# A two-block transformer on one core: stage boundaries rebuilt (row scales behind the matmuls, output units bank by bank, first units tile by tile)

## The chip, the core and the metric

The kernel runs on one core of a Trainium2 chip. TensorE multiplies matrices into PSUM, VectorE and ScalarE work elementwise on SBUF and PSUM, GpSimd does a few elementwise operations and some DMAs, and the queue of SyncE issues the weight loads. The metric is device time in microseconds; before the change it is 2071.95 us, the median of three runs (2069.97 to 2077.83). TensorE's clock has two levels, 1.2 and 2.4 GHz; the profile shows the granted clock as a share of the higher one.

## What is computed

256 tokens of 1024 features go through two layers of a first model and two layers of a second, all in fp32. Shortened:

```python
h = layer_norm(x)
for l in range(2):                       # first block
    h = layer_norm(ALPHA * h + mixer(h) @ w_out[l])        # convolution, GQA, SGU and MLA branches
    up = depthwise_conv(h @ ffn_w_up[l])                   # width 3, 5632 columns
    h = layer_norm(ALPHA * h + (silu(up[..., :2816]) * up[..., 2816:]) @ ffn_w_down[l])
x = h
for i in range(2):                       # second block; rms_norm(x) = x * rsqrt(mean(x*x) + 1e-6) * gain
    x = x + 0.5 * swiglu(rms_norm(x), ffn1_wi[i], ffn1_wo[i])
    x = x + (ssd_pool_mixer, swa_attention)[i](rms_norm(x))
    q = rms_norm_per_head(rms_norm(x) @ xattn_wq[i])       # 4 heads of 256
    x = x + softmax(q @ mem_k.T / 16) @ mem_v @ xattn_wo[i]
    x = x + 0.5 * swiglu(rms_norm(x), ffn2_wi[i], ffn2_wo[i])
```

## The kernel before

The stream `x` lies token-major in SBUF, two row tiles `tt` of 128 tokens by 1024. Each weight matrix comes in units of 1 MB through a ring of three `raw` buffers. A unit is split into two fp32r parts: ScalarE rounds it to `w_hi` (`split`, 128x2048), then VectorE subtracts it to `w_lo`. Every product is three matmul passes (hi x hi, hi x lo, lo x hi). Splits run up to two units ahead of TensorE; the split of the second unit of a stage is done on VectorE at the boundary (`split_late`).

A stage begins with its input feature-major: `xt_hi` and `xt_lo`, eight tiles `k` of 128 features by 256 tokens. `turn` transposes `z` (the normalised stream) in 16 transposes into banks 0 to 3 (bank k // 2), `take_stream` on ScalarE makes the high parts with the gain as a scale per partition, `take_stream` on VectorE the low parts. `pair_fm` or `up_pair` then multiplies one unit: first all eight `k` of the left 128 columns, then all eight of the right ones (48 matmuls of 256 columns, `feature_major`).

A stage ends with `out_rows` or `down`: each unit adds 24 matmuls of 512 columns to banks 4 to 7, one bank for each row tile `tt` and half `h`. Within a unit the order is row tile, then the unit's two 128-row parts, then half. After the last unit `residual` (VectorE) adds each bank to `x`.

Between the two lies a norm. In the first block (`norm` with tag mix or ffn) it is a LayerNorm: bn_stats, bn_aggr, square root on ScalarE, `z` = (x - mean) / deviation, and GpSimd (`apply_wide`, four operations of 128x1024) multiplies `z` by the gain and adds the bias to make the next residual `x`, as soon as `z` is there. After the last such norm VectorE does this itself, and an RMS norm follows. In the second block it is an RMS norm: ScalarE squares and sums each row tile, root, VectorE reciprocal and scaling into `z`.

In a feed-forward stage 11 chunks of 256 columns follow each other: gate unit, up unit, and the down unit of the chunk before. In the second block ScalarE takes Silu straight from the gate's bank, VectorE multiplies by the up bank and splits the product. In the first block a convolution of three taps lies in front. Cross-attention (`xattn`) projects queries (four units), normalises each head with `head_norm` (squares, mean by a matmul, root, reciprocal of 128x256 on VectorE, product), then does four heads of scores, exponentials, transposes and values.

The order on every engine is the order of the code; semaphores do the rest.

Of the kernel before, what the change touches and what calls it, by code (L numbers as in the profile page):

```python
# [22 lines left out]
ALU = mybir.AluOpType  # L23
# [221 lines left out]
def attention_heads(kind, buf, l=0):  # L245
# [22 lines left out]
    else:  # L268
        for h in range(MEM_HEADS):
# [5 lines left out]
                out=(0, 128), tile=2 * h, first=True, last=True, scale=1.0 / 16, slope=None, h=h))  # L275
# [7 lines left out]
def mixed_block_kernel(nc, inp, consts, mem_dram, out, upto=None):  # L283
# [6 lines left out]
    with ExitStack() as ctx:  # L290
# [33 lines left out]
        rsum = sb("rsum", [P, 2, TT])  # L324
        zero = sb("zero", [P, HALF], mybir.dt.bfloat16)
# [170 lines left out]
        stored = sem("stored")  # L496


        RESIDUAL = {("mix_norm_2", l): (f"ffn1.{l}", 0.5) for l in range(2)}
        RESIDUAL |= {("xattn_norm_2", 0): ("ssd.out", 1.0), ("xattn_norm_2", 1): ("swa.out", 1.0)}  # L500
        RESIDUAL |= {("ffn2_norm_2", l): (f"xo{l}", 1.0) for l in range(2)}
        RESIDUAL |= {("ffn1_norm_2", 1): ("ffn2.0", 0.5), ("store", 0): ("ffn2.1", 0.5)}
        RESIDUAL |= {("mix", l): (f"m{l}.out", None) for l in range(2)}
        RESIDUAL |= {("ffn", l): (f"conv{l}", None) for l in range(2)}


# [77 lines left out]
        def _(pe):  # L584
# [44 lines left out]
            def stream_tile(k):  # L629

                while stream_due and stream_due[0][0] <= k:
                    taken(stream_due.pop(0)[1])
# [18 lines left out]

            def pair_fm(unit, b, name):

                w = weights(unit, (KT, 256))
                dst = claim(b, name)
                first = First()
                for j in range(2):
                    ins = feature_major(dst[:, T * j:T * j + T], w, P * j, P, first)
                ins.then_inc(bank_full[b], 1)
# [10 lines left out]
            def turn(src, tag):  # L670
# [3 lines left out]
                for tt in range(TT):  # L674
                    pe.wait_ge(z_ready, seen.next(z_ready))
                    for k in range(KT):
                        ins = pe.transpose(bank[k // 2][:, T * (k % 2) + P * tt:T * (k % 2) + P * tt + P],  # L677
                                           src[:, tt, P * k:P * k + P], ident)
                        if tt == TT - 1 and k % 2:
                            ins.then_inc(bank_full[k // 2], 1)  # L680

            def turned(tag):

                assert not stream_due
                stream_due.extend((2 * b, f"{tag}.t{b}") for b in range(4))
# [3 lines left out]
            def out_rows(units, tag, bias=None):  # L689
# [9 lines left out]
                for u, unit in enumerate(units):  # L699
# [4 lines left out]
                    for tt in range(TT):  # L704
                        for r in range(2):
                            for h in range(2):
                                b = 4 + 2 * tt + h
                                for p, (s, v) in enumerate(PASSES):
                                    ins = first(mm(bank[b][:, :], act[s][:, u % 2, r, P * tt:P * tt + P],  # L709
                                                   w[v][:, r, HALF * h:HALF * h + HALF],  # L710
# [1853 lines left out]
```

## Time and profile before

| | |
|---|---|
| time, median of 3 | 2071.95 us (2069.97 to 2077.83) |
| profiled execution: span | 2080.7 us, 31025 instructions |
| TensorE busy | 1932.7 us (93%) |
| VectorE busy | 1285.5 us (62%) |
| ScalarE busy | 892.0 us (43%) |
| GpSimd busy | 101.8 us (5%) |
| chain that ended last | TensorE 84%, VectorE 10%, ScalarE 3%, GpSimd 1% |
| mean granted clock of TensorE | 0.933 |

The chain is followed back from the last instruction, at each step to what released it. A stage is long (some 190 us for a feed-forward), so the 40 slices of the page hide the boundaries; they have to be read in windows of 20 to 40 us. In the chain "PE bank L639" are projection matmuls, L799 and L709 output matmuls, and each row gives the start, the length and the work.

### The profile page before, as it was taken

To read this page: it belongs to the slowest core of one execution; us is meant where nothing else is said; L and a number is where in the kernel's file an instruction comes from. 1 tells how busy PE (TensorE), PEld (TensorE's weight loads), DVE (VectorE), ACT (ScalarE), POOL (GpSimd) and SP (SyncE) were. 2 spreads that over 40 slices of the span, in tenths; PEclk is the share of its full clock that TensorE was granted. 3 is DMA by queue.
4 is the path that set the end of the run, shared out by engine and by line. 5 is a ranking of instruction groups with operands and counts; after the bars stand their busy time and mean duration, and the time that the engine had idled before them with its cause. 6 is when DMAs were issued, how large, how long until landed. Compare 5 with 4: busy or idle time off the path is not lost.

```text
span 2080.7 us, 31025 instructions
## 1 busy us (share of the span) xinstructions
PE 1932.7 (93%) x12412; PEld 1724.3 (83%) x12412; DVE 1285.5 (62%) x1559; ACT 892.0 (43%) x1076; POOL 101.8 (5%) x79
## 2 busy tenths in 40 slices
PE   7989799978979997999988999999999988999999
PEld 7966699976679997998986788999899875688998
DVE  5786877777687776555646556555555557565555
ACT  5444444434444443334543354333433444444332
POOL 0300200020020000000041000000000000000000
PEclk9987899988889998999986999999999995899999
DMA  9531355542135554555531434555455430224553
GB/s 299 186 111 50 134 182 181 183 133 102 61 122 182 188 189 131 185 190 168 161 105 61 142 142 151 189 185 181 162 182 182 164 119 21 100 87 160 187 189 126
DMA packets 226642, 310.78 MB, mean 149 GB/s; under 512 B 6598, under 2 KB 199398, under 8 KB 225926
## 3 DMA queue, kind: packets, MB, share of 16 engines
q1 hardware_dynamic: 223750, 298.06, 42.4%
q0 software_dynamic: 2528, 10.14, 1.5%
q10 hardware_dynamic: 288, 1.52, 0.2%
q8 instruction: 53, 0.87, 0.2%
q14 instruction: 23, 0.19, 0.0%
HBM read 306.56 MB, written 3.15 MB: 149 GB/s over the span
## 4 chain that ended last, share of the span: by engine, by line
PE 84%; DVE 10%; ACT 3%; issue 1%; POOL 1%; DMA 0%; DVEq 0%; ACTq 0%
PE bank L639 47%; PE bank L799 17%; PE bank L709 7%; PE bank L648 3%; PE bank L864 2%; PE bank L836 2%; DVE w_lo L1655 2%; DVE work L1652 1%; DVE x L1652 1%; PE bank L850 1%; DVE work L1655 1%; ACT mix L1303 1%; PE bank L1108 1%; ACT w_hi L1193 1%; DVE work L2231 1%
## 5 line engine op out<-in xcount | busy, mean ns | idle before, releaser
L1655 DVE TENSOR_TENSOR w_lo<-raw,w_hi 128x2048 fp32r<-128x2048 f32 x280 | 646.3, 2312 | 513.2 <-ACT w_hi L1193 513.0
L1193 ACT ACTIVATE w_hi<-raw 128x2048 fp32r<-128x2048 f32 x280 | 533.2, 1905 | 813.0 <-PE bank L639 532.4
L639 PE MATMUL bank<-xt_hi,w_hi 128*128 128x256 f32 x2752 | 791.8, 288 | 37.0 <-DVE xt_lo L1655 24.9
L639 PE MATMUL bank<-xt_lo,w_hi 128*128 128x256 f32 x2752 | 785.8, 286 | 0.0
L639 PE MATMUL bank<-xt_hi,w_lo 128*128 128x256 f32 x2752 | 785.4, 285 | 0.0
L639 PEld LDWEIGHTS bank<-xt_hi,w_hi 128*128 128x128 f32 x2752 | 535.4, 195 | 47.0 <-DVE xt_lo L1655 17.0
L639 PEld LDWEIGHTS bank<-xt_lo,w_hi 128*128 128x128 f32 x2752 | 535.3, 195 | 3.1 <-issue 0.7
L639 PEld LDWEIGHTS bank<-xt_hi,w_lo 128*128 128x128 f32 x2752 | 534.9, 194 | 0.0
L799 PE MATMUL bank<-w_hi,act_hi 128*128 128x512 f32 x528 | 206.4, 391 | 0.0
L799 PE MATMUL bank<-w_lo,act_hi 128*128 128x512 f32 x528 | 206.2, 390 | 0.0
L799 PE MATMUL bank<-w_hi,act_lo 128*128 128x512 f32 x528 | 205.4, 389 | 0.0
L799 PEld LDWEIGHTS bank<-w_hi,act_lo 128*128 128x128 f32 x528 | 99.1, 188 | 21.1
L799 PEld LDWEIGHTS bank<-w_hi,act_hi 128*128 128x128 f32 x528 | 99.4, 188 | 19.8 <-DVE act_lo L1655 0.9
L799 PEld LDWEIGHTS bank<-w_lo,act_hi 128*128 128x128 f32 x528 | 99.4, 188 | 18.3
L1652 DVE SCALAR_TENSOR_TENSOR work<-bank,par,work 128x255 f32<-128x255 f32 (+2 forms) x212 | 92.4, 478 | 25.7 <-ACT work L1342 18.4
L1193 ACT ACTIVATE work<-bank 128x512 f32<-128x512 f32 (+6 forms) x96 | 51.5, 545 | 117.0 <-PE bank L850 56.3
L709 PE MATMUL bank<-w_hi,act_hi 128*128 128x512 f32 x224 | 89.5, 399 | 6.7 <-ACT work L1475 3.0
L709 PE MATMUL bank<-w_lo,act_hi 128*128 128x512 f32 x224 | 88.8, 397 | 0.0
L709 PE MATMUL bank<-w_hi,act_lo 128*128 128x512 f32 x224 | 88.7, 396 | 0.0
L836 PE MATMUL bank<-work 128*128 128x256 f32 (+3 forms) x192 | 64.5, 509 | 19.9 <-DVE work L1655 9.1
L1342 ACT ACTIVATE work<-bank,par 128x256 f32<-128x256 f32 x88 | 44.5, 555 | 64.6 <-PE bank L639 64.6
L677 PE MATMUL bank<-con,mix 128*128 128x128 f32 x192 | 34.2, 341 | 40.4 <-DVE mix L1824 26.0
(256 smaller groups left out, 1874.0 us busy)
## 6 DMA issues: line engine op xcount, KB each, us to landing
raw<-in_ffn_wi SPq DMA_DIRECT2D x88, 1024.0 KB, 5.0
raw<-in_ffn_w_up SPq DMA_DIRECT2D x44, 1024.0 KB, 5.1
raw<-in_ffn_wo SPq DMA_DIRECT2D x44, 1024.0 KB, 4.8
raw<-in_ffn_w_down SPq DMA_DIRECT2D x22, 1024.0 KB, 5.3
raw<-in_w_in SPq DMA_DIRECT2D x14, 1024.0 KB, 5.3
raw<-in_ssd_in_proj SPq DMA_DIRECT2D x14, 1024.0 KB, 5.1
raw<-in_mem_wkv SPq DMA_DIRECT2D x9, 1024.0 KB, 8.4
raw<-in_w_out SPq DMA_DIRECT2D x8, 1024.0 KB, 5.0
```

The costliest lines, as they stand in the source:

```text
L639: ins = first(mm(dst, w[s][:, k, c0:c0 + m], xt[v][:, k, :], start=k == 0 and p == 0, stop=k == KT - 1 and p == 2))
L648: ins = first(mm(dst, xt[s][:, k, P * tt:P * tt + P], w[v][:, k, c0:c0 + n], start=start and k == 0 and p == 0, stop=k == KT - 1 and p == 2))
L677: ins = pe.transpose(bank[k // 2][:, T * (k % 2) + P * tt:T * (k % 2) + P * tt + P], src[:, tt, P * k:P * k + P], ident)
L709: ins = first(mm(bank[b][:, :], act[s][:, u % 2, r, P * tt:P * tt + P], w[v][:, r, HALF * h:HALF * h + HALF], start=u == 0 and r == 0 and ...
L799: ins = first(mm(bank[b][:, :], act[s][:, c % 2, j, P * tt:P * tt + P], w[v][:, j, HALF * h:HALF * h + HALF], start=False, stop=True, skip ...
L836: ins = mm(bank[b][:, at:at + n], d["q"][t][c], d["k"][c][:, 0:n], start=c == 0, stop=c == len(d["k"]) - 1)
L850: ins = pe.transpose(bank[b][:, dst:dst + P], prob[:, h % prob.shape[1], d["at"][t] + P * s:d["at"][t] + P * s + P], ident)
L864: ins = mm(bank[b][r:r + m, T * c + q0:T * c + T], v[s], prob_t[:, h % 2, T * s:T * s + T - q0], start=s == 0, stop=s == TT - 1 or d["keys ...
L1193: return act.activation(dst, src, ACT.Copy)
L1342: ins = act.activation(dst[:, c % 2, j, :], bank[b][:, T * j:T * j + T], ACT.Identity, scale=par[:, cw, at], bias=par[:, cb, at])
L1652: return dve.scalar_tensor_tensor(out=out, in0=in0, scalar=scalar, in1=in1, op0=op0, op1=op1)
L1655: return dve.tensor_tensor(out=out, in0=in0, in1=in1, op=op)
```

## The change

- `turned_at`: tile k of the turned stream now lies in bank 2 (k // 4) + k % 2, so that the first four tiles need only the left half of `x`. The transposes go half a row tile at a time.
- The last output unit is done bank by bank (`rows_of` for each row tile and half; `finish_rows`), and `residual` too.
- For five norms (`DEFERRED`: before ffn2.0, ffn1.1, ffn2.1 and both cross-attentions) `x` itself is transposed, partly between the last output matmuls. The row factor is applied later: in a feed-forward it is broadcast by two matmuls (`rb`), VectorE multiplies the gate's bank by it into `f_gate` before Silu, and the residual uses half the factor (`rhalf`) in place of 0.5. In cross-attention it cancels in the head norm; the variance gets a term for it (`vcol`).
- Cross-attention has no `head_norm`: queries keep only the gain, sums of squares are matmuls of one column, and the factor per row and head (`qscale`) is the scale of the exponential.
- The first norm of the second block is merged into the LayerNorm ahead of it (`both_g`, `both_b`); VectorE makes `x` afterwards.
- `apply_wide` waits for the split of the third unit of the stage (`behind`).
- `split_late` comes after the stream's low parts (in the deferred norms between the first and second residual blocks).
- While tiles arrive, the first unit is done tile by tile for both column halves (`both_tiles`); ScalarE and VectorE take turns on the two halves of a bank.
- The last store is in four parts.

```diff
+        DEFERRED = [("ffn2_norm_2", 0), ("ffn1_norm_2", 1), ("ffn2_norm_2", 1), ("xattn_norm_2", 0), ("xattn_norm_2", 1)]
+        ORDER = [(tt, h) for tt in range(TT) for h in range(2)]
...
+            def both_tiles(dst, w, first):
...
+                for k in range(KT):
+                    stream_tile(k)
+                    for j in range(2):
+                        for p, (s, v) in enumerate(PASSES):
+                            ins = first(mm(dst[:, T * j:T * j + T], w[s][:, k, P * j:P * j + P], xt[v][:, k, :],
+                                           start=k == 0 and j == 0 and p == 0, stop=k == KT - 1 and p == 2,
+                                           skip_group_check=True))
...
+            def finish_rows(tag, bank_done):
...
+                def part(tt, h):
+                    taken(f"{tag}.{tt}{h}")
+                    turn_half(x, tt, h)
+
+                for i in range(4):
+                    bank_done(*ORDER[i])
+                    if i == 2:
+                        for b in range(4):
+                            claim(b, f"{key[0]}{key[1]}.t{b}")
+                        part(0, 0)
+                part(0, 1)
+                part(1, 0)
+                part(1, 1)
...
+                squares_of(0)
+                if (tag, l) in DEFERRED:
+                    take_stream(f"{tag}{l}", lambda k: par_col(tag, KT * l + k))
+                squares_of(1)
+                deviations(0, TT)
...
+                if (tag, l) in DEFERRED:
+                    residual(tag, l, 0, 0)
+                    late_split()
+                    residual(tag, l, 0, 1)
+                    residual(tag, l, 1, 0)
+                    residual(tag, l, 1, 1)
+                    take_stream(f"{tag}{l}", lambda k: par_col(tag, KT * l + k))
...
+                def gate(c, turn):
+
+                    b, n = names.of[f"{tag}.g{c}"]
+                    dve.wait_ge(bank_full[b], n if turn is None else turn + n)
+                    tt_(f_gate[:, c % 2, :, :], two(bank[b][:, :]), spread(rb[:, :], 2),
+                        ALU.mult).then_inc(bank_drained[b], 1)
...
                 pool.wait_ge(wide_in, seen.next(wide_in, 0))
+                pool.wait_ge(z_ready, seen.next(z_ready, z_count))
+                pool.wait_ge(unit_split, place[behind][3] + 1)
                 for tt in range(TT):
-                    pool.wait_ge(z_ready, seen.next(z_ready))
```

VectorE at the boundary from the first cross-attention layer's feed-forward (ffn2.0) to the next feed-forward (ffn1.1), before (`x` is the stream, `mix` holds `z`, `w_lo` is a weight split, `xt_lo` the low parts of the turned stream):

```order
L1652 SCALAR_TENSOR_TENSOR x<-bank,x 128x512 x4
L1823 RECIPROCAL rs<-sd 128x1
L1824 TENSOR_SCALAR mix<-x,rs 128x1024
L1823 RECIPROCAL rs<-sd 128x1
L1824 TENSOR_SCALAR mix<-x,rs 128x1024
L1655 TENSOR_TENSOR w_lo<-raw,w_hi 128x2048
L1652 SCALAR_TENSOR_TENSOR xt_lo<-bank,par,xt_hi 128x256 x8
L1655 TENSOR_TENSOR w_lo<-raw,w_hi 128x2048 x2
L1655 TENSOR_TENSOR work<-work,bank 128x512
```

and now:

```order
L1789 SCALAR_TENSOR_TENSOR x<-bank,rhalf,x 128x512
L1792 TENSOR_TENSOR w_lo<-raw,w_hi 128x2048
L1789 SCALAR_TENSOR_TENSOR x<-bank,rhalf,x 128x512 x3
L1789 SCALAR_TENSOR_TENSOR xt_lo<-bank,par,xt_hi 128x256 x8
L2033 RECIPROCAL rcol<-sd 128x2
L2035 TENSOR_SCALAR rhalf<-rcol 128x2
L1792 TENSOR_TENSOR w_lo<-raw,w_hi 128x2048 x2
L1792 TENSOR_TENSOR work<-bank,rb 128x512
L1792 TENSOR_TENSOR work<-work,bank 128x512
```

The two scalings are gone, the split has moved up among the residual blocks, the reciprocal stands behind the low parts and a product with `rb` before that with the up bank.

VectorE at the boundary from the second convolution feed-forward to the second block, from the last bn_aggr on, before:

```order
L1732 BN_AGGR mv<-bn 128x2
L1737 RECIPROCAL rs<-sd 128x1
L1738 TENSOR_SCALAR mix<-x,mv,rs 128x1024
L1655 TENSOR_TENSOR mix<-mix,wide 128x1024
L1655 TENSOR_TENSOR x<-mix,wide 128x1024
...
L1823 RECIPROCAL rs<-sd 128x1
L1824 TENSOR_SCALAR mix<-x,rs 128x1024
L1655 TENSOR_TENSOR w_lo<-raw,w_hi 128x2048
L1652 SCALAR_TENSOR_TENSOR xt_lo<-bank,par,xt_hi 128x256 x8
```

and now:

```order
L1885 BN_AGGR mv<-bn 128x2
L1979 TENSOR_SCALAR mix<-x,mv,rs 128x1024
L1889 RECIPROCAL rs<-sd 128x1
L1979 TENSOR_SCALAR mix<-x,mv,rs 128x512 x2
L1859 CAST xt_hi<-mix 128x512
L1792 TENSOR_TENSOR xt_lo<-mix,xt_hi 128x512
...
L1792 TENSOR_TENSOR w_lo<-raw,w_hi 128x2048
L1792 TENSOR_TENSOR x<-mix,wide 128x1024
L1792 TENSOR_TENSOR x<-x,wide 128x1024
...
L2033 RECIPROCAL rcol<-sd 128x2
L2035 TENSOR_SCALAR rhalf<-rcol 128x2
L1792 TENSOR_TENSOR w_lo<-raw,w_hi 128x2048 x2
```

The products with `wide` (gain and bias) have moved behind the stream and its split, but still stand ahead of the third unit's split.

TensorE from the last output unit of ffn2.0 on, now (before, 24 output matmuls were followed by 16 transposes of `mix`):

```order
L887 MATMUL bank<-w_hi,act_lo 128x512
L716 MATMUL bank<-con,x 128x128 x4
L887 MATMUL bank<-w_hi,act_hi 128x512
L887 MATMUL bank<-w_lo,act_hi 128x512
L887 MATMUL bank<-w_hi,act_lo 128x512
L887 MATMUL bank<-w_hi,act_hi 128x512
L887 MATMUL bank<-w_lo,act_hi 128x512
L887 MATMUL bank<-w_hi,act_lo 128x512
L716 MATMUL bank<-con,x 128x128 x12
L683 MATMUL bank<-xt_hi,w_hi 128x256
```

Four of the 16 transposes stand ahead of the last bank's six matmuls, and they read `x`.

## Rows read from the trace of the kernel before

**Rows 1.** Chain of the whole span; columns: start us, us, what.

```profile
1600.99 11.51 PE bank L639 x96
```

**Rows 2.** Chain around the boundary from ffn2.0 to ffn1.1.

```profile
1451.77 7.52 PE bank L799 x33
1459.32 1.38 DVE x L1652 x2
...
1461.95 1.28 ACT L1304
...
1465.96 2.20 DVE w_lo L1655
...
1469.09 11.87 PE bank L639 x96
```

**Rows 3.** Timeline there; start us, us, engine line op out<-in xcount [idle before <-releaser].

```profile
1464.67 1.06 PE L677 MATMUL bank<-con,mix 128*128 128x128 f32 x8 [1.99 <-DVE mix L1824]
...
1466.49 3.03 ACT L1221 ACTIVATE xt_hi<-bank,par 128x256 fp32r<-128x256 f32 x8 [1.52 <-PE bank L677]
1468.08 3.22 DVE L1652 SCALAR_TENSOR_TENSOR xt_lo<-bank,par,xt_hi 128x256 fp32r<-128x256 f32 x8
```

**Rows 4.** Chain around the first LayerNorm boundary (first mixer to convolution feed-forward).

```profile
208.25 1.30 DVE x L1652 x2
...
209.65 1.30 DVE bn L1730 x2
...
214.95 2.94 DVE mix L1738
...
224.75 2.72 DVE xt_lo L1655
```

**Rows 5.** Timeline at the same boundary.

```profile
214.02 0.81 DVE L1738 TENSOR_SCALAR mix<-x,mv,rs 128x1024 f32<-128x1024 f32 x1
...
214.98 2.35 POOL L2298 TENSOR_TENSOR x<-mix,wide 128x1024 f32<-128x1024 f32 x1 [67.56 <-DVE mix L1738]
...
218.66 3.76 ACT L1221 ACTIVATE mix<-bank,par 128x256 f32<-128x256 f32 x8 [4.37 <-PE bank L677]
...
227.39 0.41 DVE L1718 CAST xt_hi<-mix 128x512 fp32r<-128x512 f32 x1
...
227.84 0.69 DVE L1655 TENSOR_TENSOR xt_lo<-mix,xt_hi 128x512 fp32r<-128x512 f32 x1
```

**Rows 6.** Chain around the start of the second block.

```profile
788.15 1.24 DVE x L1655
...
795.00 13.37 PE bank L639 x96
```

**Rows 7.** Chain of the whole span: first matmuls after two LayerNorm boundaries.

```profile
227.61 13.71 PE bank L639 x96
...
434.10 23.11 PE bank L639 x168
```

**Rows 8.** Chain in the first cross-attention.

```profile
1224.31 0.60 ACT work L1193
...
1236.48 0.44 PE bank L850 x4
1236.91 1.74 PE bank L864 x8
...
1245.94 18.66 PE bank L709 x81
```

**Rows 9.** Windows at two boundaries; us, busy by engine (PE PEld DVE ACT POOL), PEclk, DMA, GB/s.

```profile
988.00:990.00 2.00, 1.09 (x8) 0.86 (x8) 2.00 (x2) 1.41 (x4) 0.00 (x0) 1.00 0.00 0
...
1196.00:1198.00 2.00, 0.80 (x4) 0.45 (x3) 2.00 (x5) 2.00 (x6) 0.00 (x0) 0.50 0.05 12
```

**Rows 10.** Timeline of VectorE in the first mixer, GpSimd working beside it.

```profile
88.33 3.98 DVE L1655 TENSOR_TENSOR w_lo<-raw,w_hi 128x2048 fp32r<-128x2048 f32 x1 [2.93 <-ACT w_hi L1193]
```

**Rows 11.** The page's costliest groups: the convolution taps and like operations.

```profile
L1652 DVE SCALAR_TENSOR_TENSOR work<-bank,par,work 128x255 f32<-128x255 f32 (+2 forms) x212 | 92.4, 478 | 25.7 <-ACT work L1342 18.4
```

More of the change, by code:

```diff
@@ L655, in pair_fm @@
                 dst = claim(b, name)
[L656 to L659, printed above, removed]
+                both_tiles(dst, w, First()).then_inc(bank_full[b], 1)
             def pair_tm(unit, b, name):
@@ L675, in turn @@
                     pe.wait_ge(z_ready, seen.next(z_ready))
[L676 to L682, printed above, removed]
-                assert not stream_due
-                stream_due.extend((2 * b, f"{tag}.t{b}") for b in range(4))
+                    for h in range(2):
+                        turn_half(src, tt, h)
@@ L687, in _, with turned @@
+            def turned(tag, biased=False):
+                assert not stream_due
+                for k in range(KT):
+                    b, half = turned_at(k)
+                    if biased and k % 2 == 0:
+                        stream_due.append((k, None))
+                    elif not biased:
+                        stream_due.append((k, f"{tag}.t{b}" if half else None))
             act = (act_hi, act_lo)
@@ L781, in ffn_any @@
                 up_pair(1, 2, None)
+                if scaled:
+                    pe.wait_ge(row_ready, seen.next(row_ready))
+                    claim(1, f"{tag}.rb")
+                    for tt in range(TT):
+                        ins = mm(bank[1][:, P * tt:P * tt + P], rcol[:, tt:tt + 1].broadcast_to([P, P]), ident,
+                                 start=True, stop=True)
+                    ins.then_inc(bank_full[1], 1)
                 for tt in range(TT):
@@ L1156, in xattn, with square_sums @@
                 turned(f"xattn_norm_2{l}")
+                def square_sums(h):
+                    pe.wait_ge(sq_ready, seen.next(sq_ready))
+                    b = 4 + h % 2
+                    claim(b, f"xn{l}.ms{h}")
+                    for tt in range(TT):
+                        for c in range(2):
+                            ins = mm(bank[b][:, tt:tt + 1], x_sq[:, 2 * h + c, P * tt:P * tt + P],
+                                     cst("mean256")[:, 0:1], start=c == 0, stop=c == 1)
+                    ins.then_inc(bank_full[b], 1)
                 for j in range(4):
@@ L1785, in residual @@
                 name, factor = RESIDUAL[tag, l]
[L1786 to L1793 removed]
+                b = full(f"{name}.{tt}{h}")
```

411 lines of the change are left out of this document (272 added, 139 removed).

## The prediction

> **What bounds the kernel now.** I read the shares of the page and its chain first: TensorE carries the chain nearly everywhere, so only places where it stands still are worth anything. In the loops of the six feed-forward stages the chain is matmuls without a gap: 96 matmuls of up-projections in 11.51 us [rows 1], then 24 of down-projection at 7.52 / 33 = 0.228 us [rows 2], 5.47 us. Nothing there can be gained. Next I read the chain across the joints. From the last output matmul (E) to the first matmul of the next stage (F) the reader should see only VectorE, ScalarE and transposes.
>
> RMS joints (seven). In the one between the two feed-forwards, [rows 2]: the last unit's first 9 matmuls end at 1459.3, when the first residual row block starts; 15 more end at E = 1459.3 + 15 x 0.228 = 1462.7. F is 1469.09, so F - E = 6.4. The other joints of this kind give the same 6.4. In it lie squares, a table load (1.28), square root, scaling, transposes, then a weight split of 2.20 that VectorE does ahead of the stream's low parts.
>
> LayerNorm joints (four; the very first stage start is covered by the memory projections). In the first [rows 4], E = 208.15 + 15 x 0.228 = 211.55, F = 227.61, so 16.1. Four VectorE instructions are stretched while GpSimd works beside them, each by 2.0 to 2.1 us; two are shown: a scaling takes 2.94 for 0.81, a subtraction 2.72 for 0.69 [rows 4, 5]; between them lie a split and a cast. Together 8.5 us. Before the second block's first norm VectorE also applies gain and bias itself (1.24 us, four times) [rows 6] and a second norm follows; F is 795.0 against E = 780.1 (the same count of matmuls after the first residual block), 14.9 us [rows 6].
>
> **The change, part by part.**
>
> A. Five RMS joints lose the norm from their path (stream turned unscaled, row factor applied behind). Work, from E of the old order: the bank-by-bank order completes the banks after 6, 12, 18, 24 matmuls in place of 9, 12, 21, 24, so the last bank is as late as before, plus the four transposes put ahead of the last group: 1.06 / 8 = 0.13 each [rows 3], 0.5 us. VectorE: block 1 at 1458.7 to 1459.4, the moved split 1459.5 to 1461.8 (its ScalarE half ends by 1459.5), blocks 2 and 3 to 1463.2, block 4 from 1463.4 (bank full) to 1464.1 (0.69 each, half of 1.38 [rows 2]). TensorE has turned tiles 0 to 3 by 1464.2. ScalarE tile 0: 3.03 / 8 = 0.38; VectorE 3.22 / 8 = 0.40 [rows 3]; two handoffs and the matmul's own: F = 1465.15 against 1469.09. Gain 3.95. Tiles then come every 0.43 (the two engines alternate over two banks) while TensorE, now taking both column halves at each tile, uses 6 x 0.12 = 0.72: no stall, where the first two units took 11.87 for 11.51, gain 0.35. Five times 4.3 = 21.5.
>
> What is late next: on ScalarE the second squares, table load and root, under 3 us, now stand between the stream and the third unit's split. They end near F + 5.5, the split's two halves by F + 9.7; TensorE wants that unit at F + 11.5 plus the zeroing matmuls. Hidden, with 3 us to spare. The row factors are then broadcast by two matmuls of 128 columns in each RMS feed-forward: nearest rows, transposes of that shape at 0.13 each and the 256-column pair of fp32 matmuls below at 0.43; I take 0.45 with the wait, bounds 0.2 to 1.0. Three joints here: -1.35. A = 20.1.
>
> B. The two RMS joints that keep their norm (before the mixers): the split leaves the path (2.20) and tiles 0 to 3 are handed over half a row block earlier, but block order costs a little: F = E + 4.35. The split then ends 0.5 us before it is wanted. Gain 2.05, twice 4.1.
>
> C. Three LayerNorm joints. VectorE in the new order, from E = 211.55: last block 212.55 to 213.2, statistics to 213.9, aggregate 214.15 (1.30 for two halves [rows 4]), first scaling 0.81 to 214.95, two half scalings to 216.0. Transposes for tiles 0 to 3 at 216.1 to 216.7, ScalarE 2 x 0.47 [rows 5], VectorE cast and subtraction 0.42 + 0.69, F = 219.0 = E + 7.45. Gain 8.6 each, 25.8. The moved split ends at F + 5.5 and is wanted at F + 5.76: just in time, bound 0 to 1 us late.
> The four GpSimd instructions are not gone but wait for the split of the third unit. In the first mixer the trace already shows them at F + 7: a split of 3.98 us for 2.29 [rows 10], and TensorE there keeps its pace, so for the second mixer I take 0. For the two convolution feed-forwards nothing shows it. From F + 7.8 VectorE has one split, 8 taps (0.48 each [rows 11]), products and operand parts (0.69 + 0.42 + 0.69) and another split before TensorE wants the first down-projection at F + 24: 10.4 of work and 8.5 of blocking in 16.2 us if everything is serial, 2.7 us too late; if the taps, which read PSUM, are not blocked, nothing. I take 0, bounds 0 to 8.5 a joint.
> The Trainium skill (SBUF — State Buffer, "SBUF: two separate sides") says that GpSimd and those VectorE operations that run in a two-port mode or read two SBUF inputs share one port pair, "an exclusive lock, not a bandwidth split". The 2.94 beside GpSimd's 2.35 agrees. The rule speaks against this part: what is moved blocks again where it lands. By it the PSUM-fed taps go free, which gives the 0; without that the sum would lose 2.7 twice.
>
> D. Before the second block: F = E + 7.45 here too, 787.55, gain 7.45. But VectorE still owes the four products (5.0 us), and ScalarE squares them before it splits the third unit: products end F + 10.5, root F + 12.1, split F + 16.3, wanted F + 13.9. So 2.1 to 2.5 us come back as a stall, and TensorE starts the third unit at F + 16.4 = 803.95 against 809.3. D = 5.4.
>
> E. Cross-attention, two. Before: from the end of the last query projection (1224.3) to the output projection (1245.94) 21.65 us [rows 8]: copy, square, mean, root, reciprocals on VectorE, products, then scores. Without head norms: square and four one-column matmuls, scores from +1.2. TensorE's own work is 4 heads x (1.74 values, as much for the scores, 0.44 transposes) = 15.7 [rows 8]; followed hand (exponential from +4.25 because the table load waits for the scores) values end at +17.7, output at +18.4. Gain 3.25. One-column matmuls are not in the trace: between 4 x 0.13 and the 0.86 of the pairs they replace (two of 256 columns, 0.43 each); I take 0.53, three more per stage, gain 1.0. E = 2 x 4.3 = 8.6.
>
> F. Clock. After long gaps the granted clock falls to half (1.2 for 2.4 GHz), seen at 1196 but not at 988 after gaps of equal length [rows 9]. First units then take 13.71 or 13.37 for 11.5, and the first 168 matmuls of the second mixer 23.11 for 20.2 us [rows 6, 7]. Outside D that is 10 us of this trace. Gaps of 2.5 us should not drop it, those of 7.5 may, as the 6.4 ones did in two of seven. I expect 3 to stay: 7.
> The Trainium skill (TensorE: Matmul & The Clock Gate, "HAM oscillation") says an idle gap re-throttles and sustained work releases. The row at 988 says a gap with transposes in it need not. By the rule each of the three remaining gaps of C costs its 2 us, 6 for my 3.
>
> Left at nothing: the gate product that replaces a read in each RMS chunk (0.69 on VectorE, which waits several us in each 16.98 us chunk; the chunk's operand is due a whole chunk later); other exponential scales; the start (second unit's split about 1 late, both halves together about 1 earlier); the smaller last transfers.
>
> Sum on the profiled execution: 20.1 + 4.1 + 25.8 + 5.4 + 8.6 + 7 = 71 off 2080.7. This execution, 2080.7 us by its span, is 8.8 longer than the median of the timed ones, though its span excludes what lies around it; that is about what the clock drops come to, so I credit the timed runs with 3 for F: 67 off 2071.95 = 2005.
>
> **Rivals.**
> 1. GpSimd's work blocks again in the open. For: the stretched rows [rows 4, 10] show blocking wherever the two meet, and VectorE is the source of each unit. Against: the first mixer. If all 8.5 us show in three joints: 2005 + 25 = 2030; if 2.7 in two, 2010.
> 2. What the joint gives is taken back by the third unit everywhere, as in D: its split stands behind second squares and root in five joints. For: D's arithmetic. Against: 3 us of slack. If ScalarE's stream is slow (each tile waiting for VectorE's, 0.8 rather than 0.43) the slack goes and each joint loses 3 to 4: 2005 + 5 x 4 + 15 for late second splits in B and C = 2040.
> 3. Slower. In the four RMS feed-forwards gate product, Silu, product, cast and subtraction become one serial chain in a loop that had no gap: 0.69 + 0.6 + 0.69 + 0.42 + 0.69 plus handoffs = 3.2 us per chunk, 44 chunks. If it lay open wholly: 141 more, 2146. It decides from 67 / 44 = 1.5 us per chunk. Against: TensorE's 16.98 us per chunk, and the operand is due more than 10 us after it is made.
> 4. It doesn't shorten: the joints' F stays because the last bank, not the norm, was late. The order above excludes it for C (8.5 us of blocking are plain).
>
> **How the numbers follow.** Forecast as worked out, with its own range 1994 to 2017: 0.74. Rival 1 0.10, rival 2 0.09, rival 3 0.04, rival 4 and other 0.03. The range goes from all terms at their good ends (square sums free, no clock drop, timed runs gain all of F: 1992) to rival 1 at full price, 2030. About 10 us is what measurement can tell from no change (0.5%). Faster holds the forecast, rivals 1 and 2: 0.94; same, a partial rival 3 or 4: 0.02; slower 0.04.
>
> **What would show it.** Between last output and first projection matmul 2.5 us in five joints, 4.4 in two, 7.5 in four; VectorE's scaling 0.81 again there; GpSimd stretching splits inside the next stage, with TensorE not waiting at the first down-projection; one wait of 2 to 3 us at the third unit of the second block's first feed-forward; 18 us from last query projection to output; loops still at 16.98. Wrong if the loops lengthen, if TensorE waits for the third unit in the five joints, or if the gaps of C exceed 9.

## The result, and the profile after

The changed kernel takes 2020.21 us (median of 4 runs, 2019.93 to 2022.33) against 2071.98 (4 runs, 2069.97 to 2077.83): 0.9749 of the time, 95% interval 0.9732 to 0.9767, so 51.8 us less, give or take 3.7. The forecast was 2005, the range 1992 to 2030. All medians here leave out one execution, of the kernel of experiment 3, that took 3779.65 us at a mean granted clock of 0.496. The profiled execution has a span of 2017.5 us, 63.2 less than that of the kernel before. The loops are what they were: in the chain of the changed kernel (start us, us, what)

```profile
1969.38 5.47 PE bank L887 x24
1974.85 11.51 PE bank L660 x96
```

11.51 us of up-projections and 5.47 of down-projection, as in [rows 1, 2]. The gate product inside the loop costs nothing.

**RMS joint without a norm in its path.** The chain of the joint between the two feed-forwards, which answers to [rows 2]:

```profile
1410.74 0.78 PE bank L716 x7
...
1411.60 0.48 ACT xt_hi L1335
...
1412.11 0.49 DVE xt_lo L1789
...
1412.63 0.48 ACT xt_hi L1335
...
1413.13 0.49 DVE xt_lo L1789
...
1413.67 6.01 PE bank L683 x48
...
1425.44 0.44 PE bank L867 x4
...
1426.85 1.15 PE bank L660 x8
```

Table load, squares, root, scaling and split are gone from it. TensorE's last transposes begin at 1410.58 in the timeline, 0.23 behind the last output matmul (the chain gives them from its end), and the next projection at 1413.67: 3.09 us, where the prediction's working gives 1.95. Before, the same distance was 6.6 (the prediction had estimated 6.4). The chain passes through two of ScalarE's tiles and two of VectorE's before TensorE moves, though its first matmul reads the first tile alone. The timeline of the same place (the bracket is the idle time before, and what ended it):

```profile
1412.11 2.68 DVE L1789 SCALAR_TENSOR_TENSOR xt_lo<-bank,par,xt_hi 128x256 fp32r<-128x256 f32 x6 [0.58 <-ACT xt_hi L1335]
...
1413.67 0.39 PE L683 MATMUL bank<-xt_hi,w_hi 128*128 128x256 f32 x1 [1.43 <-DVE xt_lo L1789]
```

VectorE makes a low tile every 0.45 us (2.68 / 6), the first by 1412.6. TensorE starts with the end of the third. The row factors' four records take 0.44 (0.45 in the prediction).

**RMS joint that keeps its norm**, before ssd, in the chain:

```profile
942.02 1.28 ACT L1424
...
943.84 0.76 DVE mix L2013
...
945.81 0.56 PE bank L716 x3
...
946.40 0.48 ACT xt_hi L1335
...
947.93 0.50 DVE xt_lo L1789
...
948.52 3.59 PE bank L669 x28
```

The last output matmul begins at 942.29 and the next instruction could follow 0.23 later, so this is 6.0 us, against 6.6 before by the same count and 4.35 in the prediction. The table load of 1.28 is still there, and where the split of 2.20 stood, transposes and tiles stand now.

**LayerNorm joint**, before the first convolution feed-forward, which answers to [rows 4, 5]:

```profile
209.48 0.69 DVE mix L1979
...
210.31 2.60 PE bank L716 x11
...
214.44 0.70 DVE xt_lo L1792
...
215.28 6.72 PE bank L683 x39
```

The subtraction of 2.72 is 0.70 again. From last output matmul (206.84) to first projection it is 8.4 us here, 7.25 and 8.0 at the next two, against 16.2 before; predicted 7.45. The transposes of this joint ran at the low clock, those of the second (7.25) at the full one. GpSimd now begins at 222.90, where it began at 214.98; the timeline there:

```profile
222.90 2.41 POOL L2523 TENSOR_TENSOR x<-mix,wide 128x1024 f32<-128x1024 f32 x1 [74.94 <-DVE w_lo L1792]
...
225.25 2.29 DVE L1792 TENSOR_TENSOR w_lo<-raw,w_hi 128x2048 fp32r<-128x2048 f32 x1 [2.52 <-ACT w_hi L1302]
...
225.39 4.40 POOL L2524 TENSOR_TENSOR x<-x,wide 128x1024 f32<-128x1024 f32 x1
...
227.46 1.78 DVE L1789 SCALAR_TENSOR_TENSOR work<-bank,par,work 128x255 f32<-128x255 f32 x4
...
232.86 2.53 DVE L1827 CAST act_hi<-work 128x512 fp32r<-128x512 f32 x1
```

Of the four only one meets VectorE at VectorE's cost here (a cast, 2.53 for 0.43). One is itself stretched, 4.40 for 2.4, by a split that began first, and the taps keep their 0.45 beside GpSimd. In the third joint a split (4.03 for 2.29) and the cast (2.52) pay. TensorE waits for none of it: from third unit to last output matmul both convolution feed-forwards take 175.43 us, before and now.

**Before the second block** the third unit is late, as forecast. In the chain:

```profile
757.73 2.37 DVE x L1792 x2
...
762.83 1.91 ACT w_hi L1302
...
764.83 2.30 DVE w_lo L1792
...
767.18 2.89 PE bank L660 x22
```

Products, squares, ScalarE's half of the split, VectorE's half, then TensorE, 15.9 us after its first projection matmul (751.31); forecast 16.4.

**Cross-attention**, in the timeline, against [rows 8]:

```profile
1176.00 1.90 PE L1262 MATMUL bank<-con,work 128*128 128x1 f32 x16
...
1188.79 0.60 ACT L1302 ACTIVATE mix<-bank 128x512 f32<-128x512 f32 x1 [1.13 <-PE bank L960]
1189.28 0.56 ACT L1520 ACTIVATE work<-bank,nmax,qscale 128x256 f32<-128x256 f32 x1
...
1191.39 0.66 PE L946 MATMUL bank<-con,work 128*128 128x128 f32 x4 [0.47 <-DVE work L2163]
...
1196.23 0.47 PE L787 MATMUL bank<-w_hi,act_hi 128*128 128x512 f32 x1 [0.73 <-issue]
```

From the last query projection (1176.00) to the output projection it is 20.2 us, against 21.65 before and 18.4 forecast. The square sums show as 16 records for two heads, 0.86 us a head, where I had put 0.53. The last head's exponential stands behind a result copy, and the output projection waits for a bank.

**Clock and the mixers.** Both mixers ended 4.4 us sooner though nothing in them was changed. In the windows of the kernel before (us, PE and PEld busy, DVE, ACT, POOL, then the granted clock) the first mixer's attention reads

```profile
160.00:170.00 10.00, 10.00 (x34) 4.49 (x32) 7.45 (x20) 2.00 (x6) 0.00 (x0) 0.50 0.01 2
```

and in those of the changed kernel

```profile
160.00:170.00 10.00, 10.00 (x45) 5.39 (x44) 7.74 (x21) 2.04 (x7) 0.00 (x0) 0.74 0.01 2
```

Half clock (1.2 GHz) through the whole window in one; in the other TensorE is back at full clock (2.4 GHz) half-way through.

### The profile page after: what moved, and what is told of

It is laid out like the page before. It is cut to its first block, busy times and chain, and to the rows that moved or that the text cites. A ratio compares the mean times of both kernels' runs of the same rounds, so it can differ in the third digit from the quotient of the medians.

```text
span 2017.5 us, 31210 instructions
## 1 busy us (share of the span) xinstructions
PE 1909.7 (95%) x12460; PEld 1712.2 (85%) x12460; DVE 1277.4 (63%) x1585; ACT 893.4 (44%) x1076; POOL 103.2 (5%) x79
## 3 DMA queue, kind: packets, MB, share of 16 engines
q10 hardware_dynamic: 288, 1.52, 0.2%
## 4 chain that ended last, share of the span: by engine, by line
PE 85%; DVE 8%; ACT 3%; issue 2%; POOL 1%; DMA 1%; DVEq 0%; ACTq 0%
PE bank L660 43%; PE bank L887 17%; PE bank L787 8%; PE bank L683 4%; PE bank L669 3%; PE bank L960 2%; PE bank L932 2%; DVE work L1789 2%; PE bank L716 1%; ACT w_hi L1302 1%; DVE w_lo L1792 1%; PE bank L946 1%; DVE work L1792 1%; PE bank L1204 1%; DVE work L2451 1%
## 5 line engine op out<-in xcount | busy, mean ns | idle before, releaser
L660 PE MATMUL bank<-xt_lo,w_hi 128*128 128x256 f32 x2560 | 725.5, 283 | 0.0
L660 PE MATMUL bank<-xt_hi,w_lo 128*128 128x256 f32 x2560 | 725.3, 283 | 0.0
L660 PEld LDWEIGHTS bank<-xt_hi,w_hi 128*128 128x128 f32 x2560 | 492.0, 192 | 6.5 <-issue 2.4
L660 PEld LDWEIGHTS bank<-xt_lo,w_hi 128*128 128x128 f32 x2560 | 491.9, 192 | 3.0 <-issue 0.7
L660 PEld LDWEIGHTS bank<-xt_hi,w_lo 128*128 128x128 f32 x2560 | 491.8, 192 | 0.0
L1789 DVE SCALAR_TENSOR_TENSOR work<-bank,par,work 128x255 f32<-128x255 f32 (+2 forms) x212 | 92.3, 478 | 23.7 <-ACT work L1477 17.3
L1302 ACT ACTIVATE work<-bank 128x512 f32<-128x512 f32 (+6 forms) x88 | 46.8, 541 | 102.9 <-PE bank L946 46.5
L683 PE MATMUL bank<-xt_hi,w_hi 128*128 128x256 f32 x192 | 59.3, 309 | 18.4 <-DVE xt_lo L1789 10.7
```

Source lines behind the costliest of these rows:

```text
L660: ins = first(mm(dst, w[s][:, k, c0:c0 + m], xt[v][:, k, :], start=k == 0 and p == 0, stop=k == KT - 1 and p == 2))
L683: ins = first(mm(dst[:, T * j:T * j + T], w[s][:, k, P * j:P * j + P], xt[v][:, k, :], start=k == 0 and j == 0 and p == 0, stop=k == KT - ...
L1302: return act.activation(dst, src, ACT.Copy)
L1789: return dve.scalar_tensor_tensor(out=out, in0=in0, scalar=scalar, in1=in1, op0=op0, op1=op1)
```

## The experiments

Times are medians; ratios are to the kernel before, with 95% intervals.

**1. The kernel before once more** (no edit): how much of the 63.2 us is one execution's clock?

> The kernel before, unchanged, profiled a second time. The two profiles differ by 63.2 us of span, the timed runs by 51.8. Theory A (the clock): about 11 us of the profiled difference is that the first profile of the kernel before held more time at the low clock level (mean 0.933), above all in the attention of the two mixers, where 32 small matmuls took 0.61 us a pair for 0.36 in the changed kernel; the timed runs hold less of it. Then this second profile has a span of about 2069 to 2072 and a mean clock of 0.937 to 0.94, and the joints' own lengths (6.4 and 16.1 us from last output matmul to first projection) are unchanged. Theory B (the changed kernel's mixers are really shorter by 4.4 us each): span again near 2080, mixers as in the first profile.

Measured: 2072.94 us, span 2070.2, clock 0.940. The window of its first mixer from 160 to 170 us:

```profile
160.00:170.00 10.00, 10.00 (x45) 5.39 (x44) 7.95 (x21) 2.01 (x6) 0.00 (x0) 0.74 0.01 2
```

It is that of the changed kernel. Theory A holds: the mixers didn't change, the first profile of the kernel before was one of its long executions. The joints have the lengths of the first profile. Its timed ones go from 2070 at a mean clock of 0.940 to 2083 at 0.934.

**2. Another bank for the first unit** behind RMS joints.

```
-claim(0, f"{tag}.g0"); up_pair(0, 0, None)
+claim(4, f"{tag}.g0"); up_pair(0, 4, None); row_factors()   # not in ffn1.0
-pair_fm(f"xq{l}.{j}", j % 2, ...)
+pair_fm(f"xq{l}.{j}", j % 2 if j else 6, ...)               # likewise ssd, swa: bank 7
```

> The changed kernel with another destination for the first unit behind an RMS joint: bank 4, 6 or 7, which the last residual has emptied, in place of bank 0, which holds the turned tiles 0 and 2 (and the two row factor matmuls between first and second unit). Theory A (destination): in the trace the first matmul starts 1.08 us after the first low tile, with the third low tile's end, because its own bank is the one those tiles are read from. Then first matmul minus last output matmul falls from 3.4 to about 2.4 us before ffn2.0, ffn1.1, ffn2.1 and both cross-attentions, the loops' third unit moves with it, 0.3 to 0.9 before ssd and swa: in all 5 to 6 us, 2020.2 to 2014.5. Theory B (the first matmul needs the tiles themselves at that pace): no change, 2020; the start moves but the first unit stretches by as much.

Measured: 2014.59 us (0.9709, 0.9683 to 0.9734), 5.6 less. In its timeline of the joint between the feed-forwards:

```profile
1414.81 0.35 PE L683 MATMUL bank<-xt_hi,w_hi 128*128 128x256 f32 x1 [0.50 <-DVE xt_lo L1796]
```

The last transposes begin at 1412.65, so 2.16 us for 3.09, and TensorE idles 0.50 for 1.43. Theory A holds. A little comes back in the first unit: at the third unit the gain is 0.99 us in cross-attention, 0.82 in the feed-forwards and 0.33 before ssd.

**3. GpSimd early again** in the changed kernel.

```
-pool.wait_ge(unit_split, place[behind][3] + 1)      # the three joints
```

> The changed kernel with one part undone: GpSimd's four gain and bias instructions start at once behind the scalings again, not behind the third unit's split. Theory A (two engines shut each other out wherever they meet): GpSimd starts near 211.4 in the first such joint; its second instruction meets VectorE's first cast (0.43 becomes 2.5), third and fourth meet a subtraction and a split. First matmul of the next stage 2.1 us later in three joints, third unit 2 to 6 later each: 2020 plus 6 to 18, so 2026 to 2038. Theory B (the new order of VectorE's own work gave the gain, the blocking is cheap): within 3 us of 2020.

Measured: 2040.76 us (four executions; 0.9848, 0.9817 to 0.9879), 20.6 more, above the range I gave. VectorE's stream in the first joint:

```profile
215.52 2.58 DVE L1859 CAST xt_hi<-mix 128x512 fp32r<-128x512 f32 x1 [2.63 <-ACT mix L1338]
218.14 2.71 DVE L1792 TENSOR_TENSOR xt_lo<-mix,xt_hi 128x512 fp32r<-128x512 f32 x1
220.78 2.60 DVE L1859 CAST xt_hi<-mix 128x512 fp32r<-128x512 f32 x1
```

Three instructions in a row pay 2.15, 2.02 and 2.18 us, together 6.35. Here two stand ahead of the first projection and the third holds up the first unit; counted at the third units, the three joints take 4.7, 6.7 and 6.5 us more, 17.8 in all. Only the first GpSimd instruction runs beside nothing. Theory A, and dearer than I had it.

**4. GpSimd late in the kernel before**, nothing else.

```
+if behind is not None: pool.wait_ge(unit_split, place[behind][3] + 1)
```

> The kernel before with that one part alone: GpSimd waits for the split of the next stage's third unit in the three LayerNorm joints. Theory A: the four stretched VectorE instructions (2.0 to 2.1 us each) were the 8.5 us; all come back at each joint and none is paid later: 2072 less 25, 2047 (from 2045 to 2051). Theory B (most of the 8 us per joint of the changed kernel came from overlapping residual, statistics and scaling): 2060 or more.

Measured: 2046.66 us (0.9874, 0.9844 to 0.9904), 26.1 less. Its chain in the first joint, with the old order of residuals, statistics and split:

```profile
209.78 0.83 DVE mix L1738
...
210.74 2.38 PE bank L677 x10
...
215.50 6.56 PE bank L639 x37
```

From the first transposes to the first projection it is 4.76 us, 4.97 in the changed kernel, both with transposes at the low clock; from the first pair of residuals (204.01) 11.5. This one wait is most of term C, and half of the whole change. In the second joint, where both kernels ran their transposes at the full clock, last output matmul to first projection is 7.8 us here and 7.25 in the changed kernel, so the finer order of VectorE's work adds 0.5. Theory A holds.

**5. The split back in the path** of the six joints that keep a norm.

```
-take_stream(...); late_split()
+late_split(); take_stream(...)
```

> The changed kernel with one part undone in the six joints that keep their norm: VectorE splits the second unit ahead of the stream's parts again, not behind them (2.2 us). Theory A (from the trace: VectorE idles 2.7 us there in the LayerNorm joints and 0.75 in the two RMS joints, waiting for transposes and ScalarE's first tile): nothing in four joints, 1.45 in two, 2020 plus 3. Theory B (the prediction's own step, 2.2 us off the path wherever the split is moved): 2.2 in six joints, 2020 plus 11 to 13.

Measured: 2023.61 us (0.9754, 0.973 to 0.9778), 3.4 more than the changed kernel. The interval doesn't tell that from nothing; the trace does. The chain before ssd:

```profile
946.23 2.20 DVE w_lo L1792
948.43 0.41 DVE xt_lo L1789
...
949.96 0.36 PE bank L669
```

From the first transposes (944.82) to the first projection it is 5.14 us for 3.78, 1.36 more; in the first LayerNorm joint 4.97 for 4.97. Theory A holds: a split of 2.2 us fills time in which VectorE would wait anyway. How much of it depends on the clock: VectorE idles 2.71 us in the first LayerNorm joint of the changed kernel, with slow transposes, but 1.52 in the second, with fast ones, and there the split costs 0.6 (4.38 for 3.78), where theory A had nothing.

**6. First units by column half again**, not tile by tile.

```
-if not stream_due:
+if True:
     for j in range(2): ins = feature_major(...)
```

> The changed kernel with the first units taken column half by column half again, not tile by tile: TensorE then uses 0.36 us per tile in the first half, under the 0.43 to 0.54 at which the tiles come. By that its first half ends with the eighth tile in place of running behind it: first unit some 0.5 to 1.0 us longer at eleven stages, 2020 plus 5 to 10 (the span of 2017.5 likewise). Rival: the first unit's start waits for a bank that is emptied with the third tile, so the stream is already ahead: under 2 us.

Measured: 2024.80 us (2 runs; 0.9761, 0.9725 to 0.9797), span 2024.5. The span's 7.0 more are mostly not this edit's: 5.7 of them are there before the first joint, where its windows show the first mixer at 0.50 and 0.57 for 0.74 and 0.92. In the joint between the feed-forwards first and second unit take 11.78 us together for 6.01 + 5.76. The rival holds there: no gain of 0.35. It does not hold where tiles come in pairs, by a cast and a subtraction of 128x512 each. The chain in the first LayerNorm joint, its first unit at full clock:

```profile
223.16 0.70 DVE xt_lo L1792
...
223.91 9.62 PE bank L660 x78
```

The first unit, begun at 220.81, is still waiting for the fourth pair of tiles; it takes 6.80 us, where the changed kernel's, at full clock in the third LayerNorm joint, takes 5.83. The first mixer's has 6.79 for 5.83 likewise. Four LayerNorm joints and the first stage are of this kind, some 1 us each, though the one before the second block waits for its third unit either way. So the median's 4.6 us, from two executions, agrees with theory A in these stages and with the rival in the rest.

**7. Square sums twice.**

```
-for tt in range(TT):
+for tt in (0, 1, 0, 1):
```

> The changed kernel with the one-column square sums of cross-attention issued twice (8 matmuls for 4 per head, same result). I had put four at 0.53 us; the trace shows 0.86 for four. Theory A (each costs 0.21 us of TensorE, set by its 128-row weight load of 0.19 and not by its one column): between the query projections 1.74 us stand in place of 0.86, so 8 x 0.87 = 7 us more in the span. Theory B (the 0.86 is mostly the switch between projections and sums, paid once): under 2 us more.

Measured: 2026.06 us (2 runs; 0.9775, 0.9753 to 0.9798), span 2023.6: 6.1 more. The span mixes in the clock (the joint before swa ran at full clock in this execution and gave 1.9 back, the first cross-attention lost some). The second cross-attention, at full clock in both, is the clean place: 3.5 us more for four heads, 0.88 for each one's four matmuls. Theory A holds; a matmul of one column costs about 0.2 us here. That its weight load sets this was not tested.

**8. All that the traces pointed to** (2, and four more edits).

```
 split(); +gate(0, None) ahead of the second split()      # ScalarE's copy of the row factors likewise
+act.activation(unused, eps[:, 0:1], ACT.Sqrt)            # at the start of each RMS joint; Exp before cross-attention
-if h >= 2: result(h - 2)
+if h >= lag: result(h - lag)                             # lag 3 in cross-attention, otherwise 2
-claim(4 + 2 * tt + h, ...) for all four, then the units
+if u == 0: claim(b, ...)                                 # each where it is first written
```

> The changed kernel with five more edits. (1) The other destination bank for the first unit behind RMS joints, measured alone at 5.6 us. (2) In those three feed-forwards the first gate product and the row factor's copy stand ahead of the second of the two splits: the third unit, which waited in the trace of the kernel with edit 1 alone for splits and gate product, starts about 0.7 us sooner. (3) The square root's table (1.28 us) is loaded by a throwaway square root at the start of each RMS joint, in ScalarE's idle time: both joints that keep their norm lose 1.28 us of path, 2.5 in all; the exponential's likewise before each cross-attention, 0.3 each. (4) In cross-attention the fourth head's exponential stands ahead of the first head's result copy: 0.5 each. (5) The output rows' accumulators are claimed when each is first written, so that the first matmul doesn't wait for the last value head's copy: 0.6 at six stages, 3.6. Sum with 5.6: 2020.2 less 15, 2005 (2001 to 2009). Rival: what edits 3 to 5 free is taken by the next wait of the same place (split of the third unit, last head's operand): 2011 or more.

Measured: 2002.49 us (0.9662, 0.9645 to 0.968), 17.7 less than the changed kernel, inside what was expected. The chain before ssd is without its table load:

```profile
942.39 0.76 DVE x L1804
...
943.23 1.16 ACT mix L1426 x2
...
944.41 0.30 ACT sd L1429
...
947.20 2.73 PE bank L670 x18
```

From the last residual (942.39) to the first projection it is 4.81 us, where the changed kernel has 5.80 (942.72 to 948.52). But the kernel of experiment 2, which still has the table load in its chain, has 4.82 (948.70 to 953.52):

```profile
953.52 0.36 PE L669 MATMUL bank<-w_hi,xt_hi 128*128 128x256 f32 x1 [0.63 <-DVE xt_lo L1796]
```

So the whole 1.0 is the other bank's, and hiding 1.28 us of table load brought nothing here: the second row tile's squares, root and scaling, which wait for the last residual, had run beside it and now are the path. The 17.7 us come from five edits at once; only the first was measured alone.

**9. Matmuls on zeros in TensorE's gaps**, in the changed kernel.

```
+busy(3, 13)      # before each LayerNorm joint's transposes
+busy(7, 9)       # behind them
+busy(0, 18)      # before each mixer's attention
```

> The changed kernel with matmuls on a tile of zeros put where TensorE waits, into banks that are empty then: 13 before the transposes and 9 behind them in each of the four LayerNorm joints, 18 before the attention of each mixer (0.21 us each at full clock). They change no result and delay nothing while they fit the gaps (3.3, 2.3 and 4.5 us). Theory A (the gaps let the granted clock fall): in the trace the granted clock stays at 1.00 at 210 to 220 and 482 to 498 us (0.53 and 0.5 to 0.57 in the changed kernel), the first unit of the first joint takes 6.0 us for 7.8, its transposes 1.3 for 2.6, and each mixer's attention is 3 to 6 us shorter: 2020.2 less 9 to 15, so 2005 to 2011. Theory B (the clock falls for another reason, or matmuls on zeros don't count): 2020 to 2023.

Measured: 2018.39 us (0.9736, 0.9721 to 0.9752), 1.8 less, where I expected 9 to 15. The joints did as theory A said (the first: transposes and first unit 1.97 and 5.89 us). The first mixer did not:

```profile
150.00:160.00 10.00, 7.97 (x23) 4.33 (x22) 9.79 (x28) 3.16 (x12) 0.00 (x0) 0.55 0.00 1
160.00:170.00 10.00, 10.00 (x35) 4.81 (x34) 7.88 (x21) 2.18 (x8) 0.00 (x0) 0.50 0.01 2
```

The clock is still up at first (0.83 from 140 to 150 us, for 0.55), falls at the attention's next wait, and stays down longer than in the changed kernel's trace (0.50 from 160 to 170 for 0.74): the output projection begins at 190.26 us for 185.0. One trace doesn't show that the zeros did the second part. From third unit to last output matmul the first mixer takes 126.5 us here, and in the twelve traces without zeros there anything from 119.4 to 125.5, three of them with 0.50 from 160 to 170 too.

**10. The edits of 8 and 9 together.**

> Both kernels' edits together. If they touch different time, the gains add: 2005 less what the filling matmuls give alone (9 to 15 by their theory A), 1990 to 1996. If they give nothing alone, 2005 to 2008.

Measured: 2001.62 us (0.9656, 0.964 to 0.9671), where 1990 to 1996 was expected. In its trace the first mixer takes 124.7 us and the second 117.7, the shortest of all.

**11 and 12. The edits of 8, and zeros in the joints alone**, twice.

> The combined kernel with the filling matmuls in the four LayerNorm joints alone, none before the mixers' attention. In the trace of the kernel with all of them the joints gained 2.8, 1.6, 1.5 and 1.2 us and both mixers lost 4 to 5 (the clock fell later in them, and stayed down longer). Theory A (both readings hold): 2002.5 less 7, 1995.5 (1994 to 1999), the granted clock 1.00 in the first units of all four joints and the mixers' attention as in the kernel without filling. Theory B (what the joints keep, the stage behind them loses, since the clock falls at the next gap all the same): 2001 to 2003.

> The combined kernel with the filling matmuls in the four LayerNorm joints, once more. Its first six executions lay between 1995.7 and 2007.7 (median 1998.0) and the profiled one was the longest, with a mean clock of 0.948 where the others had 0.955 to 0.958. Theory A (a real gain of 3 to 6 us on the combined kernel's 2002.5): median between 1996 and 2000 again, and the longer executions are those of lower mean clock. Theory B (chance of one chip): 2001 to 2004.

Measured: 1997.97 us (0.9627, 0.9603 to 0.9651) and 1996.14 (0.9624, 0.9599 to 0.9649). Its window in the first LayerNorm joint, first time:

```profile
210.00:220.00 10.00, 9.61 (x66) 7.02 (x64) 8.27 (x18) 5.85 (x10) 0.00 (x0) 1.00 0.00 0
```

and that of kernel 8 (in the second joint 1.00 against 0.83):

```profile
210.00:220.00 10.00, 7.98 (x37) 7.64 (x38) 7.12 (x13) 5.76 (x10) 0.00 (x0) 0.51 0.00 0
```

Theory A in both, with 4.5 and 6.4 us of its 7. This is the best version: 75 to 76 us under the kernel before, 22 to 24 under the changed one. The intervals of 8 and 11, and of 8 and 12, overlap, so that the zeros help rests on both medians and the rows, not on one comparison. That the zeros before the mixers cost something rests on the medians of 10 against 11 and 12 alone, 3.7 and 5.5 us for both mixers, and the intervals touch.

## Why the prediction was right, and where it was too high

Terms on the profiled executions. Each joint is counted from its last output matmul to the third unit behind it, less the 0.45 us of the four transposes that now stand ahead of that matmul; E is the rest of the two cross-attentions. The measured columns compare the changed kernel with the first profile of the kernel before and with the second (experiment 1). "Without the clock" puts in, for each joint, its length where another trace of the same order ran it at full clock.

| term | predicted | without the clock | first profile | second profile |
|---|---|---|---|---|
| A, five RMS joints | 20.1 | 14.0 | 17.3 | 17.0 |
| B, two that keep their norm | 4.1 | 1.4 | -0.5 | -0.5 |
| C, three LayerNorm joints | 25.8 | 29.9 | 28.2 | 27.5 |
| D, before the second block | 5.4 | 4.7 | 5.0 | 5.2 |
| E, cross-attention | 8.6 | 3.3 | 3.3 | 3.3 |
| sum of these | 64.0 | 53.3 | 53.3 | 52.5 |
| F, clock in the joints (the sums' difference, in them already) | 7, 3 of it credited | | 0.0 | -0.8 |
| mixers, by the clock | none | | 8.8 | -0.7 |
| start, end, rest of ssd and swa | none | | 1.1 | 0.9 |
| span | 71 | | 63.2 | 52.8 |

The second profile is the typical one: its 52.8 agree with the timed difference of 51.8. The forecast's 67 was 15 too high: A 6.1, E 5.3, F 3, B 2.7 and D 0.7 too much, C 4.1 too little. That the total still came within 15 owes something to C's surplus.

- **C is right in its cause and shown from both sides**: 26.1 us for the wait alone in the old kernel, 20.6 lost without it in the new. That the four instructions are hidden behind the third split (price taken as 0) is right in all three joints. The Trainium skill ("SBUF — State Buffer", section "SBUF: two separate sides") has the port pair go to whoever starts first, the other fully blocked. The trace agrees in both directions: VectorE's 2.53 for 0.43, GpSimd's 4.40 for 2.41, and taps fed from PSUM unharmed. Residual and statistics by halves gave 0.5 us a joint (experiment 4). What C left out is the first unit taken tile by tile, 1.0 a joint (experiment 6): the 13.71 us that the prediction's F reads as clock loss over 11.5 held the same 1.0 of waiting for tiles at full clock.
- **A failed in two steps.** The first is "F = 1465.15": I let the first matmul go with the first tile. Its own destination, bank 0, held turned tiles 0 and 2, so it waited for the third: 0.93 us at five joints at the first projection, 4.4 in all at the third unit (experiment 2). The second step, "gain 0.35" for taking tiles as they come, was nothing in these joints, since a stream that is two tiles ahead doesn't need it (experiment 6): 1.7. Together the 6.1 missing. What was to be late next was not late: TensorE reaches the third unit without a wait in all five.
- **B failed at "the split leaves the path (2.20)"**: it covered transposes and ScalarE's first tile. It is worth 1.36 and not 2.2 (experiment 5), and the wait for bank 0, not in the prediction, took 1.0 of that back (TensorE idles 1.61 us before the projection, 0.63 with the other bank). The table load of 1.28, which stands in the chain, was worth nothing either (experiment 8). As profiled, B is below 0 because the joint before swa ran at the low clock in the changed kernel's trace (first unit 8.11 us; 6.54 in experiment 7's).
- **D** is right, with its place (15.9 for 16.4 us).
- **E**: four one-column matmuls cost 0.86 us, my upper bound, not 0.53, so no gain over the pairs: 1.0 a stage (experiment 7). "Output at +18.4" left out the exponential behind a copy (0.47 of TensorE's time) and the last bank (0.73, as before); in experiment 8 projection to output is 1.8 us shorter. Of the 5.3 missing this explains 4.4; 0.4 a stage stays open.
- **F** should have been 0. The clock was low in as much of the joints' work after the change as before it, at other places: before, in the first units behind the four LayerNorm joints and of both cross-attentions; now, in three first units, before swa, and in the transposes of three joints (4.97, 4.54 and 4.97 us to the first projection for 3.78). The profiled difference owes 8.8 us to the mixers instead, which the prediction does not name: chance of one execution. That execution was 8.8 us over the timed median; that was the sign that its clock rows were not the kernel's typical ones, and I still credited 3.
- **Rivals**: 1 and 2 appear nowhere in the size given; 3 is refuted by the loops' 16.98 us, 4 by the joints.

The Trainium skill's rule on clock oscillation ("TensorE: Matmul & The Clock Gate", section "HAM oscillation") was weighed at 6 us against my 3. Of the three LayerNorm joints' first units two ran at the low level (7.80 and 7.48 us for 5.98), and with the slow transposes the clock cost these joints 5.3 us, so the rule was nearer than my row at 988; filling the gaps, with that before the second block, brought 4.5 to 6.4 us.

## What to carry to other kernels

Before counting on a matmul that starts with its first operand, look at what its destination bank still holds and who reads it. An instruction taken out of a path gives back only what it didn't cover (1.36 of a split's 2.20, nothing of a table load's 1.28): list what waits underneath, in order, and take the next arrival. And before crediting a clock loss seen in one profile, compare that execution's length with the timed median, and subtract what the same instructions take at full clock elsewhere.

## What the runs showed that was not expected

- Matmuls on zeros in TensorE's gaps held the granted clock in the four joints (1.00 for 0.51 and 0.83). Before the mixers' attention, whose next wait is 2.4 us, the clock fell all the same, only later (0.83 for 0.55, then 0.55 and 0.50). Whether they also made the mixers longer stays open: two traces with them give 126.5 and 124.7 us for the first and 123.9 and 117.7 for the second, twelve without them 119 to 125.5 for either.
- Executions of one kernel differ by up to 13 us (2070 to 2083) with their mean clock (0.940 to 0.934); between the two profiles 9.4 of 10.4 us lie in the mixers, at the same instructions.
- A matmul with one moving column and a 128 x 128 stationary operand in fp32 takes about 0.22 us and leaves two records: 16 more of them cost 3.5 us in the second cross-attention, and four cost what the two 256-column ones did that they replaced.
- GpSimd and VectorE delay each other in both directions: a GpSimd instruction of 2.4 us took 4.3 to 4.4 when a split had begun first.
